# A hybrid decoder layer on one core: key tiles handed over by head, weight splits, norm transposes and tail sums in other places of the same instruction streams

## The reference, cut to what matters

```
h = RMSNorm(x); [qA,kA,vA | qB,kB,vB | gate] = h @ w_in
A: dilated sliding-window attention, 8 heads of 64, ALiBi bias, three branches mixed
B: forgetting attention, 8 heads of 64, logit[t,s] += c[t]-c[s], c = cumsum(log sigmoid(gate))
x = x + concat(A, B) @ w_out
x = x + CrossAttn(RMSNorm(x), RMSNorm(mem))          4 heads, 256 memory tokens
x = x + relu(RMSNorm(x) @ w_up)^2 @ w_down           hidden width 4096
y = RMSNorm(x)
```

## Time and profile before

| | |
|---|---|
| median of 3 runs | 1658.94 us (1657.84 to 1661.23) |
| the profiled execution | 1661.05 us |
| its span (first to last instruction) | 1659.4 us, mean granted clock 0.993 |
| PE busy | 1616.9 us (97%) |
| PEld (weight loads) busy | 1372.5 us (83%) |
| DVE busy | 882.9 us (53%) |
| ACT busy | 644.0 us (39%) |
| prologue, to the first scores | 0 to 77 us |
| one full pair | 67.6 us |
| last pair | 548 to 614 us |

### The profile page before, as it was taken

One profiled execution on the slowest core, in us unless ns is written; L12 is line 12 of the kernel. 1 busy time (PEld: TensorE's weight loads), 2 busy tenths in 40 slices (PEclk: granted clock), 3 DMA queues, 4 the chain that ended last, 5 costly groups with the idle time before them and its releaser, 6 DMA issues.

```text
span 1659.4 us, 22259 instructions
## 1 busy us (share of the span) xinstructions
PE 1616.9 (97%) x8376; PEld 1372.5 (83%) x8376; DVE 882.9 (53%) x1511; ACT 644.0 (39%) x1082; POOL 121.7 (7%) x228
## 2 busy tenths in 40 slices
PE   5999999999999899999999999999999999999997
PEld 5788888888888788898888888888888888888886
DVE  6444444344444443663244464555555567676876
ACT  5445555455454552441133343343343331212113
POOL 0000000000000000000000002333333320000000
PEclk9999999999999899999999999999999999999999
DMA  5101010111100133052110113666666799675753
GB/s 186 51 26 28 14 40 16 26 28 27 27 20 22 34 125 108 26 152 76 51 51 1 64 51 111 216 218 213 210 210 214 261 356 358 228 274 205 261 199 152
DMA packets 153103, 204.76 MB, mean 123 GB/s; under 512 B 8208, under 2 KB 93328, under 8 KB 153008
## 3 DMA queue, kind: packets, MB, share of 16 engines
q1 hardware_dynamic: 135104, 144.95, 26.8%
q0 software_dynamic: 17920, 58.73, 10.1%
HBM read 140.61 MB, written 63.57 MB: 123 GB/s over the span
## 4 chain that ended last, share of the span: by engine, by line
PE 91%; ACT 4%; DVE 3%; issue 2%; DMA 0%; SPq 0%; DVEq 0%
PE psG L724 15%; PE psG L707 11%; PE psG L709 11%; PE psG L708 11%; PE psS L1080 9%; PE psO L872 7%; PE psO L1080 4%; PE psG L1080 4%; PE psS L820 4%; PE psG L801 3%; PE psS L736 2%; PE psS L735 2%; PE psG L1002 2%; PE psG L1004 2%; PE psG L1003 2%
## 5 line engine op out<-in xcount | busy, mean ns | idle before, releaser
L707 PE MATMUL psG<-act_hi,w_hi 128*128 128x512 f32 (+1 forms) x656 | 254.9, 389 | 2.8 <-DVE act_lo L1378 2.4
L708 PE MATMUL psG<-act_lo,w_hi 128*128 128x512 f32 (+1 forms) x656 | 254.3, 388 | 0.0
L709 PE MATMUL psG<-act_hi,w_lo 128*128 128x512 f32 (+1 forms) x656 | 254.2, 388 | 0.0
L872 PEld LDWEIGHTS psO<-V,pT 128*128 128x128 f32 x1152 | 147.1, 193 | 27.1 <-ACT pT L1187 18.4
L872 PE MATMUL psO<-V,pT 128*128 128x64 f32 x1152 | 146.4, 273 | 9.2 <-ACT pT L1187 9.2
L1187 ACT ACTIVATE pT<-psS 128x128 f32<-128x128 f32 (+7 forms) x128 | 83.5, 653 | 181.8 <-PE psS L820 181.5
L693 POOL DMA_DIRECT2D op_rows<-a_hi x112 | 60.8, 543 | 1241.0 <-DVE a_lo L1378 1205.6
L724 PE MATMUL psG<-act_hi,w_lo 128*128 128x512 f32 x360 | 151.1, 420 | 0.0
L724 PE MATMUL psG<-act_hi,w_hi 128*128 128x512 f32 x360 | 148.7, 413 | 0.0
L707 PEld LDWEIGHTS psG<-act_hi,w_hi 128*128 128x128 f32 x656 | 124.0, 189 | 28.3 <-DVE act_lo L1378 2.6
L724 PE MATMUL psG<-act_lo,w_hi 128*128 128x512 f32 x360 | 145.8, 405 | 0.0
(11 more groups left out here) (231 smaller groups left out, 3124.2 us busy)
## 6 DMA issues: line engine op xcount, KB each, us to landing
act_hi<-op_rows SPq DMA_DIRECT2D x38, 1024.0 KB, 7.5
op_rows<-a_hi POOLq DMA_DIRECT2D x112, 256.0 KB, 2.8
op_rows<-a_lo POOLq DMA_DIRECT2D x112, 256.0 KB, 3.3
act_lo<-op_rows SPq DMA_DIRECT2D x18, 1024.0 KB, 7.6
raw<-in_w_up_dram SPq DMA_DIRECT2D x32, 512.0 KB, 4.7
raw<-in_w_in_dram SPq DMA_DIRECT2D x22, 512.0 KB, 4.1
qB<-in_w_down_dram SPq DMA_DIRECT2D x8, 1024.0 KB, 9.9
act_late<-in_w_down_dram SPq DMA_DIRECT2D x8, 1024.0 KB, 10.4
```

What stands on the lines that cost most here:

```text
L707: nc.tensor.matmul(dst, sh, mh, start=(k == 0), stop=False)
L708: nc.tensor.matmul(dst, sh, ml, start=False, stop=False)
L709: mm = nc.tensor.matmul(dst, sl, mh, start=False, stop=(k == n - 1))
L872: mm = nc.tensor.matmul(psO[:, u % 2, 0:HEAD], pT[:, b * P:(b + 1) * P], V[par][:, b, h * HEAD:(h + 1) * HEAD], start=(b == 0), stop=(b == ...
```

## The change

It has five parts, and no instruction is taken out.

1. In the prologue norm transpose 3 stands behind 5 of the 8 blocks of the first half tile and not behind the whole, norm transposes 5 and 7 stand in the middle of tiles 1 and 2, and the copy of value tile 0 (vT) stands on VectorE behind the low part of first_k and not behind that of norm tile 6. In pair 0 the first piece G stands ahead of T(0).
2. The last key tile of a pair ("last", pairs 0 to 6) is taken out one head in step 0 and the other in step 1. The same is done for key tile 3 at the end of pair 6 and for tiles 4 and 5 in the last pair ("head"). New semaphores last_hi and last_out count head 0, and the QK that needs only head 0 waits for those.
3. In the last pair the split of a block of output weights stands behind PV(u) and not behind T(u), on both engines.
4. In its steps 8 to 15, both Y transposes stand ahead of PV(u), and the copy to pT is made in two: the first 4 blocks of keys on tr_half, then the rest. PV(u) begins on pT_half.
5. In the tail the variance of a token tile stands ahead of the part sum that used to be ahead of it.

```diff
@@ -108,17 +108,24 @@
...
         order.append(("T", u))
...
-        if u == 0 and has_next:
-            order.append(("last", len(PAIR_TILES) - 1))
+        if u < 2 and has_next:
+            order.append(("last", u))
+        if second is not None:
+            order.append(("head", second, 1))
+            second = None
         if complete is not None:
-            order.append(("tile", complete))
+            if kind == LAST_PAIR:
+                order.append(("head", complete, 0))
+                second = complete
+            else:
+                order.append(("tile", complete))
             complete = None
...
             if not has_next:
-                if u in Y_STEPS:
-                    order.append(("Y", 2 * Y_STEPS.index(u) + part))
+                if u in Y_STEPS and part == 0:
+                    order += [("Y", 2 * Y_STEPS.index(u) + half) for half in range(2)]
...
                 order.append(("PV", u))
                 if u + 2 == STEPS and kind == SHORT:
-                    order.append(("tile", complete))
+                    order.append(("head", complete, 0))
                     complete = None
+                if u + 1 == STEPS and kind == SHORT:
+                    order.append(("head", PAIR_TILES.index((K_, 0)), 1))
...
+        def halves_of(kind, u):
+
+            return max(0, u - (STEPS // 2 - 1)) if kind == LAST_PAIR else 0
...
             pe.wait_ge(n_lo, 2)
-            first_tile(0)
+            first_tile(0, 0, 5)
             norm_tr(TT // 2 - 1, a_hn[1])
+            first_tile(0, 5, KT)
...
-                if j:
+                if j in (1, 2):
+                    proj(j, chunk, half, 0, PRODUCTS // 2, slots)
+                    norm_tr(TT // 2 + 2 * j - 1, a_hn[1])
+                    proj(j, chunk, half, PRODUCTS // 2, PRODUCTS, slots)
...
                 if j < 2:
                     norm_tr(TT // 2 + 2 * j, a_hn[0])
-                    norm_tr(TT // 2 + 2 * j + 1, a_hn[1])
...
+                if p == 0:
+                    ahead = next(ev for ev in steps if ev[0] == "G")
+                    steps.remove(ahead)
+                    steps.insert(steps.index(("T", 0)), ahead)
...
                             mm = nc.tensor.transpose(psS[u % 2][:, b * P:(b + 1) * P], S_of(which, u)[:, b * P:(b + 1) * P], ident[:])
+                            if b == 3 and halves_of(which, u):
+                                mm.then_inc(tr_half, 1)
                         mm.then_inc(tr_done, 1)
...
                         if u == STEPS:
-                            pe.wait_ge(tile_out, body_tile(p, 3))
+                            if which == SHORT:
+                                pe.wait_ge(tile_out, body_tile(p, 2))
+                                pe.wait_ge(last_out, p + 2)
+                            else:
+                                pe.wait_ge(tile_out, body_tile(p, 3))
...
-                            if u == (3 if has_next else STEPS // 2):
+                            if u == 2 and not has_next:
+                                pe.wait_ge(tile_out, body_tile(p - 1, 3))
+                            if u == 3 and has_next:
+                                pe.wait_ge(last_out, p + 1)
+                            if u == STEPS // 2 and not has_next:
+                                pe.wait_ge(tile_out, body_tile(p, -2))
+                                pe.wait_ge(last_out, PAIRS + 2)
+                            if u == (5 if has_next else STEPS // 2 + 3):
                                 pe.wait_ge(tile_out, body_tile(p, -1))
...
-                        pe.wait_ge(pT_done, p * 16 + (u + 1))
+                        if halves_of(which, u):
+                            pe.wait_ge(pT_half, halves_of(which, u))
+                        else:
+                            pe.wait_ge(pT_done, p * 16 + (u + 1))
                         if u >= 2:
                             pe.wait_ge(o_out, p * 16 + (u - 1))
                         for b in range(qb + 1):
+                            if b == 4 and halves_of(which, u):
+                                pe.wait_ge(pT_done, p * 16 + (u + 1))
                             mm = nc.tensor.matmul(psO[:, u % 2, 0:HEAD], pT[:, b * P:(b + 1) * P],
                                                   V[par][:, b, h * HEAD:(h + 1) * HEAD], start=(b == 0), stop=(b == qb))
                         mm.then_inc(pv_done, 1)
...
-            def qk_hi_out(j, chunk, half, a):
...
-                for h in range(2):
+                for h in heads:
...
                     if kind == "T":
                         n = keys_of(which)[u] * P
+                        first = 0
+                        if halves_of(which, u):
+                            first = HALF
+                            act.wait_ge(tr_half, halves_of(which, u))
+                            nc.scalar.activation(pT[:, 0:first], psS[u % 2][:, 0:first], ACT.Copy).then_inc(pT_half, 1)
                         act.wait_ge(tr_done, p * 16 + (u + 1))
-                        nc.scalar.activation(pT[:, 0:n], psS[u % 2][:, 0:n], ACT.Copy).then_inc(pT_done, 1)
+                        nc.scalar.activation(pT[:, first:n], psS[u % 2][:, first:n], ACT.Copy).then_inc(pT_done, 1)
                         if u + 1 < STEPS or has_next:
                             exp_step(which, u + 1, p * 16 + (u + 2))
-                        if not has_next and u in OUT_STEPS:
-
-                            m = OUT_STEPS.index(u)
-                            block_hi(C_OUT + m, OUT_SLOTS[m])
+                    elif kind == "PV" and not has_next and u in OUT_STEPS:
+                        m = OUT_STEPS.index(u)
+                        block_hi(C_OUT + m, OUT_SLOTS[m])
...
                     elif kind == "last":
                         act.wait_ge(tile_done, body_tile(p, -1))
-                        qk_hi_out(LAST, *PAIR_TILES[LAST], par)
-                    elif kind == "tile" and not has_next:
-                        act.wait_ge(tile_done, body_tile(p - 1, u))
-                        qk_hi_out(u, *PAIR_TILES[u], par)
+                        qk_hi_out(LAST, *PAIR_TILES[LAST], par, heads=(u,), done=(last_hi, qk_hi)[u])
+                    elif kind == "head":
+                        act.wait_ge(tile_done, body_tile(p if has_next else p - 1, u))
+                        qk_hi_out(u, *PAIR_TILES[u], 1, heads=(ev[2],), done=(last_hi, qk_hi)[ev[2]])
...
-            def tile_rest(j, chunk, half, a, hi_count):
+            def tile_rest(j, chunk, half, a, hi_count, heads=(0, 1), hi=qk_hi, out=tile_out):
...
-                    dve.wait_ge(qk_hi, hi_count)
-                    for h in range(2):
+                    dve.wait_ge(hi, hi_count)
+                    for h in heads:
...
-                if t == TT:
+                if t == TT // 2 + 2:
 
                     dve.wait_ge(tile_done, 1)
                     tile_rest(0, *FIRST_TILES[0], 0, None)
...
+                        if not has_next and u in OUT_STEPS:
+                            m = OUT_STEPS.index(u)
+                            later_lo(C_OUT + m, OUT_SLOTS[m])
...
+                    elif kind == "head":
+                        dve.wait_ge(tile_done, body_tile(p if has_next else p - 1, u))
+                        if ev[2] == 0:
+                            tile_rest(u, *PAIR_TILES[u], 1, PAIRS + (u - 3), heads=(0,), hi=last_hi, out=last_out)
+                        else:
+                            tile_rest(u, *PAIR_TILES[u], 1, (PAIRS - 2) * 4 + (4 + QK_COUNT[u]), heads=(1,))
...
                     elif kind == "last":
                         dve.wait_ge(tile_done, body_tile(p, -1))
-                        tile_rest(LAST, *PAIR_TILES[LAST], par, p * 4 + 4)
+                        if u == 0:
+                            tile_rest(LAST, *PAIR_TILES[LAST], par, p + 1, heads=(0,), hi=last_hi, out=last_out)
+                        else:
+                            tile_rest(LAST, *PAIR_TILES[LAST], par, p * 4 + 4, heads=(1,))
...
-                    elif kind == "T" and not has_next and u in OUT_STEPS:
-                        m = OUT_STEPS.index(u)
-                        later_lo(C_OUT + m, OUT_SLOTS[m])
...
                     op_lo_out(n + 1)
+                if n == N_PARTS - 1:
+                    final_var(3)
                 part_add(n, 0)
...
                 if n == N_PARTS - 1:
-                    final_var(3)
                     final_scale(3)
                 for s in range(1, 4):
+                    t = 4 * (n - N_PARTS + 2) + s - 1
+                    if n >= N_PARTS - 2:
+                        final_var(t)
                     part_add(n, s)
                     if n >= N_PARTS - 2:
-                        t = 4 * (n - N_PARTS + 2) + s - 1
-                        final_var(t)
                         final_scale(t)
```

29 lines of the change are left out of this document (19 added, 10 removed).

## The result

| | before | after |
|---|---|---|
| median | 1660.22 us (6 runs, 1657.84 to 1661.45) | 1647.43 us (6 runs, 1645.05 to 1648.17) |
| ratio | | 0.9923, 95% interval 0.991 to 0.9936 |
| the profiled execution | 1661.05 us | 1647.2 us |
| its span | 1659.4 us | 1645.5 us |

By these medians the kernel is 12.8 us faster, where I had forecast 12.9; the forecast of the time was 1646.0 us. That is closer than the measurement can tell. The kernel before was run 32 times more beside the experiments, with medians of 1658.5 to 1658.7 us; the median of all its 38 runs is 1658.7 us, and against that the change gives 11.3 us. Nine of the 38 took over 1660.7 us, and so did the profiled execution. The sum came out about right. Several of its terms did not, and the experiments show that some of them were right for no good reason.

A forecast was written before the change was run, and what follows sets the result against it. TensorE, busy nearly all the span, was taken as the bound; only its waits, low clock and the tail could move. Terms summed to 12.9 us: 1661.05 to 1648.1, less 2.1 for the median, 1646.0 us; 8-in-10 range 1639.5 to 1652.5.

The forecast's parts named there:

- Prologue: Up to pair 0: moved transposes start tile 3 3.0 us earlier, less 1.7 for a low clock; gain 1.3 us.
- The price of 1.7 us that I had left out of the sum: First half tile: transposes ahead of the clock's rise might delay it one stretch, costing about 1.7 us; not counted.
- Pairs 0 to 5: Splitting the last key tile's copies saves 0.4 us a pair, plus 0.4 in pair 0; gain 2.4 us (0 to 3.0).
- Pair 6: Its head 0.5 us, QK(16)'s wait 1.1, the low stretch behind it 1.4; gain 3.0 us (1.5 to 4.0).
- Last pair: T(1) to the last Y transposes: 0.9 up to PV(7), 1.7 low clock, 2.1 steps 8 to 15; 4.7 us.
- half of the cases lose it ... I take 1.7 us of the 4.3: Last pair's low clock, 571.9 to 582.0: may go, costing 4.3 us now; 1.7 us taken (0 to 4.3).
- so all 3.0 us go: Last pair, steps 8 to 15: pT in halves and both Y transposes first remove all 3.0 us of pT waits.
- The wait at Y(0): Last pair: Y(0) waits for tile 5's second head, copied only behind exp(7); a new wait of about 1.5 us.
- Tail: Behind the last product: the sum fills the square root's trip, the last scale comes 1.5 us earlier (1.0 to 1.6).
- The clock holds: Rival, chance 0.17: no low clock in prologue or last pair; gain 17.2 us, 1641.7 us.
- The waits only change places: Rival, chance 0.11: second heads delay steps 2 and 3, the last pair's first half wins nothing; gain 6.7 us, 1652.2.
- The signs: Expected in the profile after: named waits gone or new, period 67.2 us a pair, klb wait over 1 us before Y.

The follow-up runs named there:

- run 32: Not a label but a count: the kernel before was run 32 times more beside the experiments, medians 1658.5 to 1658.7 us.
- experiment 2: The changed kernel with the prologue of before (norm transposes and copy of vT back in their old places; first piece G stays ahead of T(0)): 1648.51 us.
- Experiment 3: The changed kernel with query tile 1's copies and the gate weights' split ahead of the last norm copy, their rests likewise on VectorE: 1642.78 us.
- experiment 1: The changed kernel with both heads of a pair's last key tile copied out in step 0, four copies in a row on ScalarE: 1650.72 us.
- experiment 7: The changed kernel with key tile 3 copied out whole behind PV(14) at the end of pair 6, QK(16) waiting for all of it: 1646.71 us.
- experiment 5: The changed kernel with eleven unread 512-column products added behind T(5), T(6) and T(7) of the last pair, to fill TensorE's waits: 1647.74 us.
- experiment 6: The changed kernel with pT copied whole, not in halves, in steps 8 to 15 of the last pair: 1648.36 us.
- experiment 8: The changed kernel with both heads of tiles 4 and 5 copied in one go in the last pair: 1645.87 us.
- experiment 4: The changed kernel with the tail of before, the part sum ahead of the variance: 1648.55 us.
- experiment 12: The changed kernel with early query copies, last-pair head and Y copies ahead of exp(u+1) on ScalarE, and four unread products behind T(5) and T(6): 1635.36 us.
- experiment 9: The changed kernel with ScalarE's head and Y copies ahead of exp(u+1), not behind it, in the last pair: 1640.65 us.

## Why the forecast was right, and where it was wrong

That the sum met the result this closely is luck: pairs 0 to 5 gave 1.6 us more than their term, the last pair 0.9 less, and two of the last pair's three terms rest on causes that the experiments deny.

- **Prologue (1.3 forecast; 1.7 between the two profiles, 1.1 by experiment 2).** Right in mechanism and size. Tile 3 started at 45.69 (forecast 46.0) behind a wait of 3.00 us (2.9), for the query copies, and the low clock followed. Experiment 3 shows both to be one cause. Whether transposes ahead of the first rise of the clock delay it, the run can't say, since the clock had risen before them: eight stand at 21.66 us and take 1.04 us, where eight at 8.39, still at 1.2 GHz, took 1.94, and the last product ahead of them is followed 0.19 us later. The rise came at about 21.6, against 22.3 in before. The price of 1.7 us that I had left out of the sum did not come.
- **Pairs 0 to 5 (2.4; 4.0).** Right in mechanism, the size wrong: the term of 0.4 us a pair was the idle time of the earlier trace rows and a tenth. Read from start to start it is 0.61 (experiment 1). Pair 0's own piece G is what is left of the 4.0, about 0.4, as forecast. The same shows in the busy time: of the 4.0 us, 1.2 were idle and 2.9 stood as busy.
- **Pair 6 (3.0; 2.8).** The start: 0.41 us by T(3) (forecast 0.5), with the wait of 0.82 us for the second head that I had read from the order. The end: QK(16) without a wait, the low stretch gone. The sum was right, the step that gave it the credit was not: I put it down to the second head's move, but experiments 1 and 7 show that the move gives nothing here (64.54 and 64.79 us against 64.71). What is left is that the heads are counted apart, which no run took back by itself.
- **Last pair (4.7; 3.8).** Here the working failed and the number hardly shows it. The step "half of the cases lose it ... I take 1.7 us of the 4.3" for the low clock: it stayed whole, and experiment 5 shows that losing it is worth nothing in this order. The step "so all 3.0 us go" for the halves: the waits went, and experiment 6 shows that the halves have no part in the gain. The wait at Y(0) came (0.99 us, forecast 1.5), and I took it for a local price; experiment 8 shows the moved second heads to cost 1.7 us. What gained is then what is left: the weight splits behind PV(u), the Y transposes together and the heads counted apart, by 62.40 - 56.91 = 5.5 us together. None of the three was tried by itself, so how the 5.5 us are shared stays open. The ring explains at most a part. In before, a weight block's high part (1.04 us) stood on ScalarE and its low part (1.23 us) on VectorE between exp and the Y copies, but exp(8) to exp(11) did not wait for their minima there: ScalarE waited for T(7) to T(10) ahead of them, 1.21, 2.50, 1.21 and 1.22 us, so in that order TensorE had a part in what set the steps. Its low clock of 10.1 us, which nobody took away in the order of before, may be in the 5.5 us too.
- **Tail (1.5; 1.5).** Right, and for the reason given (experiment 4).
- **The rivals.** "The clock holds" priced the last pair's clock at 2.6 us more; held by force, it gave 0. In the prologue its premise was false, and worth 1.6 us when made true (experiment 3). "The waits only change places" was right in one place that I had not priced: the last pair's heads.
- **The signs and the bounds.** The signs came as named, with two small misses: the wait before Y(0) was 0.99 us where I had said over 1, and a pair took 401.15 / 6 = 66.9 us where I had said 67.2. The high bounds of the terms add up to 20.8 us, not 22, and the chances of the outcomes that I call faster to 0.95, not 0.94; nothing rests on either.

What I had missed throughout is a question: for each wait I asked what TensorE waited for, and stopped at the engine named. Going on from there, exp to minima to low part to copies to exp, closes on itself without passing TensorE in the changed order.

## What to carry to other kernels

Follow a wait back until the chain ends or closes. If it closes among other engines, their order sets the period, and neither a fuller TensorE nor a higher clock nor a finer hand-over moves the end (experiments 5 and 6: 0 us); one reordering inside the ring gave 6.8 us. A cheap way to find out is to fill the waiting engine with work that nobody needs: if the end does not move, that engine is not the bound. Price a short wait from start to start of the instructions around it, not by its idle time: 0.33 us of idle cost 0.61. And when an engine's work is pulled forward, look at which of its inputs did not move: here the query copies and the gate weights' split, left where they stood, cost 4.65 of the 5.75 us that the prologue could have given (by the medians of experiments 2 and 3).

## What the runs showed of the hardware

- In experiment 5 eleven 512-column products filled 2.3 us of TensorE's waits (0.77 us at PV(5), 1.05 at PV(6), 0.47 of the 0.99 at Y(0)), and the granted clock was 1.00 where it had been 0.50 for 10.3 us. In experiment 12 four products did it for 6.8 us.
- One and the same wait of 3.0 us in the prologue was followed by a low stretch of 3.4 us in some profiled executions, of 7 us in three (experiments 5, 6 and 9), and of none in experiment 8, where the gate tile started at 44.69 behind its 2.97 us. T(0) of pair 0 stood at 76.8 to 78.1 behind 3.4 us, at 77.9 to 78.0 behind 7 us, and at 74.7 behind none, where the gate tile also started 1.0 us earlier than in after. Runs of one kernel differ by up to 3 us; that this is their cause is likely and not shown. The stretches of experiments 9 and 8:

```profile
44.30:51.20 6.90, 5.97 (x14) 4.74 (x15) 2.14 (x4) 1.65 (x3) 0.00 (x0) 0.51 0.08 18
```

```profile
40.00:52.00 12.00, 9.03 (x40) 7.19 (x39) 5.85 (x7) 5.36 (x10) 0.00 (x0) 1.00 0.40 105
```
